# Blocks of the last head with four units, attention ahead of units on VectorE, and the residual sum of the odd tokens ahead of the last product

## What is computed

```python
mod = silu(c) @ ada_w[0] + ada_b[0]
shift, scale, gate = split(mod, 3)
h = rms_norm(x, norm_pre[0]) * (1 + scale) + shift
q, k, v, z = h @ diff_w_in            # 2048 x 8192, four parts
# per head, per block of 128 queries, masked by chunks of 64 tokens:
p0, p1 = softmax(q0 k0^T / sqrt(128)), softmax(q1 k1^T / sqrt(128))
o = (p0 - lam * p1) @ v
o = rms_norm(o, diff_subln) * 0.8 * silu(z)
y = o @ diff_w_out                    # 2048 x 2048
out = x + gate * rms_norm(y, norm_post[0])
```

## Time and profile before

| | us |
|---|---|
| median of three runs | 1972.61 |
| lowest and highest | 1970.39, 1972.65 |
| the profiled execution's own time | 1970.01 |
| its span, first to last instruction | 1968.2 |
| TensorE busy | 1894.0 (96%) |
| VectorE busy | 1407.6 (72%) |
| ScalarE busy | 804.0 (41%) |
| GpSimd busy | 800.5 (41%) |
| mean granted TensorE clock | 0.988 |

### The profile page before, as it was taken

The page is one execution under the profiler, slowest core; times in us unless marked ns, Lnnn a source line. Parts: engine busy times, 40 slices in busy tenths (PEclk is TensorE's granted clock), DMA queues, the critical chain, the costliest instruction groups (busy, mean ns, idle before and its releaser), DMA issues.

```text
span 1968.2 us, 26325 instructions
## 1 busy us (share of the span) xinstructions
PE 1894.0 (96%) x9042; PEld 1548.9 (79%) x9042; DVE 1407.6 (72%) x2059; ACT 804.0 (41%) x1504; POOL 800.5 (41%) x844
## 2 busy tenths in 40 slices
PE   4999999999999999999999999999999979999995
PEld 1478888888878888888888888888888867888884
DVE  2797878786566446778778787778778755678556
ACT  4533333333444333444444444444444434455441
POOL 2065666565545423344343534344343421134032
PEclk8999999999999999999999999999999999999997
DMA  9878888887575868776868777777868667667755
GB/s 326 257 245 293 278 287 286 277 287 243 195 244 191 289 260 259 227 237 217 246 202 243 232 230 233 218 235 219 247 202 241 217 189 230 206 227 255 259 168 214
DMA packets 407217, 473.17 MB, mean 240 GB/s; under 512 B 22598, under 2 KB 284844, under 8 KB 404396
## 3 DMA queue, kind: packets, MB, share of 16 engines
q1 hardware_dynamic: 406800, 471.43, 74.3%
q10 hardware_dynamic: 284, 0.05, 0.0%
HBM read 323.54 MB, written 147.86 MB: 240 GB/s over the span
## 4 chain that ended last, share of the span: by engine, by line
PE 84%; DVE 5%; issue 3%; SPq 2%; DMA 2%; ACT 2%; POOL 2%; DVEq 0%; POOLq 0%; ACTq 0%
PE ps L1699 27%; PE ps L1701 26%; PE ps L1700 26%; PE ps L1831 2%; PE ps L1682 1%; DVE xt L1581 1%; POOL stg L834 1%; PE ps L1805 1%; SPq L566 1%; PE ps L1850 1%; POOL sums L794 1%; DVE ub L1535 1%; SPq L432 1%; ACT ub L1115 0%; DMA h_dr<-stg 0%
## 5 line engine op out<-in xcount | busy, mean ns | idle before, releaser
L1699 PE MATMUL ps<-blk,ring 128*128 128x512 f32 x1524 | 604.3, 397 | 8.6 <-DVE cc L1326 4.0
L1701 PE MATMUL ps<-blk,ring 128*128 128x512 f32 x1524 | 595.4, 391 | 0.0
L1700 PE MATMUL ps<-blk,ring 128*128 128x512 f32 x1524 | 594.7, 390 | 0.0
L1699 PEld LDWEIGHTS ps<-blk,ring 128*128 128x128 f32 x1524 | 286.7, 188 | 70.4 <-issue 12.8
L1701 PEld LDWEIGHTS ps<-blk,ring 128*128 128x128 f32 x1524 | 286.4, 188 | 61.1
L1700 PEld LDWEIGHTS ps<-blk,ring 128*128 128x128 f32 x1524 | 286.9, 188 | 56.0
L1239 DVE TENSOR_TENSOR ring<-sums,ring 128x512 fp32r<-128x512 f32 x256 | 233.0, 910 | 98.1 <-ACT ring L954 96.3
L794 POOL TENSOR_TENSOR sums<-raw 128x512 f32<-128x512 f32 x128 | 192.0, 1500 | 260.4 <-DVE ring L1239 180.0
L954 ACT ACTIVATE ring<-sums 128x512 fp32r<-128x512 f32 x256 | 160.4, 627 | 173.7 <-PE ps L1701 172.2
L1239 DVE TENSOR_TENSOR ring<-raw,ring 128x512 fp32r<-128x512 f32 x192 | 180.0, 938 | 58.4 <-ACT ring L954 57.9
L1535 DVE TENSOR_TENSOR ub<-ubf,ub 128x1024 fp32r<-128x1024 f32 x113 | 155.0, 1406 | 80.0 <-ACT ub L1115 79.3
(11 more groups left out here) (159 smaller groups left out, 3236.7 us busy)
## 6 DMA issues: line engine op xcount, KB each, us to landing
raw<-in_diff_w_in_dram SPq DMA_DIRECT2D x64, 1024.0 KB, 7.9
d_dr<-cc SPq DMA_DIRECT2D x124, 256.0 KB, 3.2
cc<-d_dr SPq DMA_DIRECT2D x124, 256.0 KB, 4.0
ubf<-s_dr SPq DMA_DIRECT2D x113, 256.0 KB, 4.7
ada<-in_ada_w_dram SPq DMA_DIRECT2D x92, 256.0 KB, 7.0
tb<-in_diff_w_out_dram SPq DMA_DIRECT2D x32, 512.0 KB, 5.6
t_dr<-tb SPq DMA_DIRECT2D x32, 512.0 KB, 4.9
ada<-in_ada_w_dram SPq DMA_DIRECT2D x32, 512.0 KB
```

Source lines behind the costliest of these rows:

```text
L1699: MM(dst, a_hi, b_hi, start=start, stop=False, skip_group_check=True)
L1700: MM(dst, a_hi, b_lo, start=False, stop=False, skip_group_check=True)
L1701: return MM(dst, a_lo, b_hi, start=False, stop=stop, skip_group_check=True)
```

## The change

1. `x`'s last two tiles get their own semaphore `xh_last`; `finish(1, 0)` waits only for the first six, `finish(0, 2)` for the last two. The four `finish(1, p)` stand in ticks 101 to 104, one each, and the squares they rest on come two per tick in ticks 97 and 98. x's first six tiles are loaded six units apart instead of four.
2. In the last head VectorE has `out_scale` ahead of `make(u)`, and `gate` and `combine` ahead of `make(u + n0)`. Unit 6 is split one tick later.
3. `SLOTS` of blocks 0 to 3 is (1, 2, 1) instead of (1, 1, 1), and of blocks 5 to 7 (2, 2, 1) instead of (2, 2, 2). The eight blocks hold 35 units instead of 34.
4. `T_SLOTS` begins with slot 8 instead of 6 (so its last two steps fall into slots 154 and 155), w_out's loads come five slots ahead instead of six, and `scale_x2(1, t)` is one tile per slot from slot 163 on.
5. The late reload of P4's block counts on `blk_in[P4]` instead of a semaphore of its own.

```diff
-    T_SLOTS = [n for n in range(6, NA) if n % NP in (P1, P2, P4)][:8 * HEADS]
+    T_SLOTS = [n for n in range(8, NA) if n % NP in (P1, P2, P4)][:8 * HEADS]
...
-    SCALE1 = 164
+    SCALE1 = 163
...
-    SQUARES = sorted((END[q] + 1 + p, q, p) for q in COMPLETE for p in range(PAIRS))
+    SQUARES = sorted((END[q] + 1 + (p // 2 if q == LAST - 2 else p), q, p) for q in COMPLETE for p in range(PAIRS))
...
-    ROOT1, FINISH1 = END[LAST - 2] + 5, END[LAST - 2] + 7
-    SLOTS = [(1, 1, 1), (1, 1, 1), (1, 1, 1), (1, 1, 1), (1, 1, 2), (2, 2, 2), (2, 2, 2), (2, 2, 2)]
+    ROOT1 = END[LAST - 2] + 4
+    SLOTS = [(1, 2, 1), (1, 2, 1), (1, 2, 1), (1, 2, 1), (1, 1, 2), (2, 2, 1), (2, 2, 1), (2, 2, 1)]
...
+            if n == LH - LEAD - 1:
+                return n + LEAD - 1
...
-                sp.dma_start(xt[t][:, :], x[0, t * P:(t + 1) * P, :]).then_inc(xh_in, 16)
+                sp.dma_start(xt[t][:, :], x[0, t * P:(t + 1) * P, :]).then_inc(xh_in if t in XT[:TT - 2] else xh_last, 16)
...
-                t, r = divmod(n - BEGIN[9] - UR, 4)
+                t, r = divmod(n - BEGIN[9] - UR, 6)
...
-                if 0 <= n - SCALE1 < TT // 2:
-                    for t in range(2):
-                        scale_x2(1, 2 * (n - SCALE1) + t)
+                if 0 <= n - SCALE1 < TT:
+                    scale_x2(1, n - SCALE1)
...
-                    dve.wait_ge(xh_in, 16 * TT)
+                    dve.wait_ge(xh_in, 16 * (TT - 2))
+                if t == XT[TT - 2]:
+                    dve.wait_ge(xh_last, 16 * 2)
...
-                make(u)
                 maxes(LH, qb, 0)
                 if qb < HT:
                     maxes(LH, qb, 1)
+                out_scale(*last)
+                make(u)
                 if qb == 0:
                     post_low(NALL - 1)
-                out_scale(*last)
...
-                make(u + n0)
                 if qb >= HT:
                     maxes(LH, qb, 1)
                 gate(*last)
                 combine(LH, qb)
+                make(u + n0)
...
-                if v == FINISH1:
-                    finish(1, 0)
+                if v > ROOT1:
+                    finish(1, v - ROOT1 - 1)
             make(BEGIN[LAST])
-            finish(1, 1)
-            finish(1, 2)
...
-                if p == 0:
-                    finish(1, PAIRS - 1)
```

More of the change, by code:

```diff
@@ L92, in build @@
     LEAD = 2
-    ROOT1, FINISH1 = END[LAST - 2] + 5, END[LAST - 2] + 7
-    SLOTS = [(1, 1, 1), (1, 1, 1), (1, 1, 1), (1, 1, 1), (1, 1, 2), (2, 2, 2), (2, 2, 2), (2, 2, 2)]
+    ROOT1 = END[LAST - 2] + 4
+    assert ROOT1 + PAIRS == BEGIN[LAST] - 1
+    SLOTS = [(1, 2, 1), (1, 2, 1), (1, 2, 1), (1, 2, 1), (1, 1, 2), (2, 2, 1), (2, 2, 1), (2, 2, 1)]
     OUT_BANK = (0, 1, 2, 7)
@@ L296, in build @@
         y_a, y_d, yss_ok, yg_ok, y_end_ok = sem("y_a"), sem("y_d"), sem("yss_ok"), sem("yg_ok"), sem("y_end_ok")
-        gpb_in, xh_in = sem("gpb_in"), sem("xh_in")
+        gpb_in, xh_in, xh_last = sem("gpb_in"), sem("xh_in"), sem("xh_last")
         yms_ok, yr1, yrs_ok, fin, out_st = sem("yms_ok"), sem("yr1"), sem("yrs_ok"), sem("fin"), sem("out_st")
@@ L612, in _ @@
                 for z in range(2 * HEADS):
-                    if n == max(2, T_SLOTS[4 * z] - 6):
+                    if n == T_SLOTS[4 * z] - 5:
                         load_t(z)
@@ L618, in _ @@
                     load_x2(0, n - SCALE0 + 16)
-                if 0 <= n - SCALE1 + 6 < TT // 2:
+                if 0 <= n - SCALE1 + 5 < TT // 2:
                     for t in range(2):
-                        load_x2(1, 2 * (n - SCALE1 + 6) + t)
+                        load_x2(1, 2 * (n - SCALE1 + 5) + t)
                 if n == ADA0 + 16 * MODS + 8:
@@ L640, in slot @@
                     sp.wait_ge(prod, NA - 2)
-                    sp.dma_start(slotB[P4][:, :, :, :].bitcast(F32), h_dr[P4]).then_inc(blk_late, 16)
+                    sp.dma_start(slotB[P4][:, :, :, :].bitcast(F32), h_dr[P4]).then_inc(blk_in[P4], 16)
                 if pi == P3 and i + 2 < 2 * GP:
@@ L758, in _ @@
                 t = 2 * p + 1
-                sp.wait_ge(fin, 2 * p + 2 if p < PAIRS - 1 else 2 * PAIRS)
+                sp.wait_ge(fin, 2 * p + 2)
                 sp.dma_start(out[0, t * P:(t + 1) * P, :], xt[t][:, :]).then_inc(out_st, 16)
@@ L1750, in product_waits @@
                 if i == GP + PARTS_IN - 1 and pi == P4:
-                    pe.wait_ge(blk_late, 16)
+                    pe.wait_ge(blk_in[P4], 32)
             def product(n, js=range(KB)):
```

1 line of the change is left out of this document (removed).

## The result

The changed kernel takes 1985.0 us, median of 4 runs (1984.1 to 1987.5); the kernel before, beside it, 1972.5 (1970.4 to 1972.7). The ratio is 1.0068, with an interval of 1.0050 to 1.0085: slower by 12.5 us. The prediction was 1980, range 1962 to 1989.

What follows compares the result with a forecast made beforehand. The prediction saw PE held up by 16.1 us of idle time in the last head and split waits in the last chain. Terms -13.0 + 20.2 - 0.6 + 1.0 = +7.6 gave 1977.6 profiled, median 1980, range 1962 to 1989.

Steps and rivals of the forecast that it cites:

- The end: Last chain: own semaphore and odd tokens early cut PE's waits for splits and bring the last read-out sooner; -13.0 us.
- The step from 1907.6 on: VectorE before the last chain: its work up to unit 112's split, ready at 1927.8; 3.4 us of PE's wait remain.
- the 7.2 by the rule: Last chain: three VectorE passes each wait for a whole POOL product, 7.2 us instead of 5.9; the end's term -11.7.
- The order: Last head: VectorE's new order and the fourth unit remove 12 of 16 us of PE's waits if nothing else came late.
- What is late next: the loads: Last head: loads run two units ahead of PE instead of four; 33.3 us of waits against 16.1, with slow clock +20.2.
- PE 4 to 7 us for `prob` ahead of `turn`: Sign of a right forecast, blocks 4 to 6 of the last head: PE waits 4 to 7 us there.
- The clock: Last head: five waits over 3.4 us can each bring a slow piece of 1.6; 0 to +6.5, taken as +3.
- The input product: POOL's sums moved: PE's first wait of 0.65 can go, -0.6; x's last loads come later, +1.0.
- Loads nearly in time: Rival, last head: loads land near 3.2 us, so about no change, 1968.0 to 1974; chance 0.17.
- Faster: Rival, blocks 4 to 6: ScalarE's wait between exponentials doesn't come about; 1946, or 1962 with one block in two; chance 0.15.
- The end gives little: Rival, last chain: `finish(1, 3)` and unit 112 fall wholly into POOL's products, PE waits near 9; 1989, chance 0.06.
- More slow clock: Rival, last head: +28 us there instead of +20.2, total 1988; chance 0.12.

Runs made afterwards that it cites:

- e8_six_split: Changed kernel with old unit counts, unit 6 loaded first at place (0, 2), unit 8 at (1, 1), unit 112 split ahead of `finish(1, 3)`: 1939.8 us.
- e9_lead2_old: Changed kernel with old unit counts, its loads from place (1, 2) on two units ahead of TensorE instead of four: 1983.6 us.
- e2_slots_old: Changed kernel with the old counts of units in the last head, so loads run four units ahead again: 1951.2 us.
- The probe: Kernel before with five waits of TensorE, of growing length, put in where it otherwise runs without a gap; run once: 2000.5 us.
- the equal waits: One wait ahead of `turn` in block 1, compared in the kernel before, e3_end_only and e6_input_only: 3.08, 3.09 and 2.94 us.
- e3_end_only: Kernel before with only the end's part: own semaphore for x's last two tiles, odd tokens earlier, tiles six units apart: 1959.6 us.
- e6_input_only: Kernel before with only the input product's part: POOL's sums from slot 8, loads five slots ahead, one scale per slot: 1973.7 us.

## Why the prediction was right, point by point

The mechanism held: the loads came late, nearly everywhere at the places that were named, and that outweighed the gain at the end. One term, the clock, was far too small. In the profiled pair the forecast was +7.6 and the difference +14.0: +8.4 from the clock (11.4 against 3), -0.5 from idle time in the head (16.7 against 17.2), +0.3 from the end, -1.8 from what lies ahead of the last head (-1.4 against +0.4).

- **The end**, -13.0 forecast: -12.7 in the trace and -13.1 alone. The step from 1907.6 on (three pairs early, the fourth and one split behind the read-outs) held: 3.54 us of PE's wait against 3.4. On the three passes beside POOL's products, the trace of before would have shown more than its one row of 7.92 us: taken singly, the first three of those four sums start 2.2 us apart, and the last takes 1.3. POOL's product takes 1.3 us alone or beside the read-outs, and 2.27 beside VectorE's passes, by the line in the changed kernel (shortest, median, longest in ns):

```profile
L930 POOL TENSOR_TENSOR y<-y,gpb x28: 1303/2266/2287, 1785.2 to 1953.4; 128x512 f32<-128x512 f32 x28
```

  and the split beside it 2.28 instead of 1.22 (the rows of DVE above). The Trainium skill, page "SBUF — State Buffer", section "Who interferes with whom", says that such a pair of instructions shuts each other out. These rows agree: the two engines take turns, and a pass and a product together take 2.3 us, where the two alone add up to 2.5. Three such turns would be 6.8; the first pass met less of it (3.73 for the two sums, 1.4 and 2.3), hence 6.0. So it was luck that the 5.9 came out right, being worked out from a mean, and the 7.2 by the rule was 1.2 too much, since it let the first pass wait for a whole product too.
- **The order**: "12 of the 16 us would go" if nothing else came late. Alone it takes 7.6 of them (16.2 to 8.6) and 9.8 us of the median. What came late is the load of unit 6, the last of a burst, with the wait of 4.96 us in block 1; with that load ahead of the others (e8_six_split, which has the end and the input product too) idle time is 4.3, so 11.9 have gone. So the 12 was right under its condition. In the change the prediction did price that load (block 1: 3.0 us, measured 4.20).
- **What is late next: the loads.** This decided the sign, and it held: from two units of load distance 32.4 us (e9_lead2_old against e2_slots_old). Idle time came out at 33.0 against 33.3, closer than its parts, whose errors cancel: block 1 had 4.2 instead of 3.0, block 2 2.8 instead of 4.0, block 5 3.7 instead of 4.8 with its `weighted`, block 6 8.0 instead of 5.6, and the 1.0 for the first unit that reads the last head's own sums shows as no wait of its own (SP waits at most 0.5 us for such a store). In block 6 PE waits 6.83 us not at `turn` but one unit earlier, for a read-out of y on ACT, which stands behind the same late split and the exponentials; I had looked for no read-out there. So of the sign "PE 4 to 7 us for `prob` ahead of `turn`" only block 4 shows it (6.70; block 5 has 3.30), while ACT's waits of 8.2 to 10.4 us between the exponentials are there in all three. That loads from SP "took 4.7 and more" holds for the places that were looked at: the shortest of the 42 was 3.2.
- **The clock**, "0 to +6.5, taken as +3": this is the term that was mis-sized. It was +11.4 in the profiled pair. Six slow pieces fell into the last head, some 38 us at 1.2 GHz by the clock column; 11 of these lay inside PE's waits, and 27 covered its work, 3.4 to 5.4 us each. I had taken 3.4 us for each of five, and part of each hidden. The probe and the equal waits show why a fixed price was wrong. Part of the 11.4 may also be that the profile of before was a lucky one: e3_end_only and e6_input_only, whose last head is that of before, were busy there for 136.7 and 137.3 us, 2.1 and 2.7 more. Against those the clock term is 8.6 to 9.3. With +3 set to +9 the sum would be 1986, against 1985.0 measured.
- **The input product**, +0.4 forecast, +1.2 measured, not to be told from nothing. Neither of its two parts went as said: the first wait of PE is 0.93 instead of 0.65 us, not gone, and the one behind x's scales 3.99 instead of 3.40.
- **The rivals.** "Loads nearly in time" and "Faster" fell with the waits of 8 us and more on ACT. "The end gives little" fell with 3.54 us. "More slow clock", 1988, had the right direction: the truth lies between it and the forecast. The time is at the top edge of the forecast's own range, 1975 to 1985; a little more of slow clock would have put it outside.

## What to carry to other kernels

When the number of units of work per stage is changed, the places at which transfers are issued, splits made and products run all shift, and where their schedules are tied to the same table their distances to each other change without a line about it in the diff: count, for each place, how far ahead of the consumer the load, the split and the product stand before and after. An in-order engine that holds a wait for a late load in the midst of a latency-bound chain (scores, exponentials, `turn`) makes the load everyone's wait. Parts should be judged one by one: here two good ones, worth 13 and 10 us, were hidden behind one that cost 34 beside them (1985.0 - 1951.2). And where several loads go out in one burst, the one that is needed first belongs at its head: moving unit 6's there, together with one split at the end, gave 11 us more (1951.2 to 1939.8).

## What I had not expected of the hardware

The slow pieces of TensorE's clock behind a wait don't follow from the wait's length: waits of 1.92, 2.51, 3.63, 4.76 and 7.01 us were followed by 3.0, 0, 5.7, 2.7 and 3.2 us at 1.2 GHz. A longer wait also hides more: of the longest, 3.6 us were already at 1.2 GHz while PE stood. And the same wait of some 3 us in one place was followed by 36, 31 or 25 matmuls in 10 us. From these runs an estimate can take an average price, here 1.5 us a wait with a spread of 0 to 2.9; single executions with the same last head differed by 2.1 and 2.7 us of PE's busy time there. What decides it in the single case stays open; nothing here was run that could tell.
